# State tables transposed between two gate projections, state products ahead of output products, other PSUM banks

## Chip, cores and metric

The kernel runs on one core of one Trainium2 chip. The metric is the device time of one execution in microseconds (us), from the runs shown below; lower is better.

## The reference

Two blocks in sequence on x (512 tokens, 1024 wide). The first is a mixer (gated linear recurrence plus a Fourier mix) and a mixture of 16 experts with chosen tokens. The second, where the change lies, is

```python
h = rms_norm(x, norm_gain)
q, k, v, z_a, u, z_s, g_a, g_s = split(h @ w_in)         # g_a, g_s get a bias
y_a = (band_attention(q, k, v, rel_bias) * silu(z_a)) @ w_attn_out
y_s = gelu(s5_ssm(u, ...))     # 32 groups of 16 channels, 64 complex diagonal states each
y_s = glu(y_s @ w_glu + b_glu)
y_s = (y_s * silu(z_s)) @ w_ssm_out
x = x + (sigmoid(g_a) * y_a + sigmoid(g_s) * y_s) @ w_out
return rms_norm(x, final_gain)
```

## The kernel before

**Place in the program.** The mixer and the experts come first; the second block starts late. After the projections of u, q, k and v, TensorE (PE) runs a loop of 12 steps (L1147). Step i computes two gate projections, `gate{2i}` and `gate{2i+1}`. These are z_a, z_s, g_a and g_s in slices of 128 columns. A projection is 24 matmuls (L696 to L698: for each of eight tiles of 128 rows, low part by high, high by low, high by high). The two projections of a step share one unit of weights.

**Work between the gates.** The attention of a pair of heads and the state-space model of a quarter `c` of its channels (128 of 512) are spread over steps 0 to 8:

- At the end of an odd step p: `pair_probs` (probabilities transposed), `ssm_lags` (L1106, product `lags_p`), `pair_values`, `pair_scores` of the next pair.
- At the end of an even step with c = i/2: `ssm_tables(c)` (L1097, eight 128x128 transposes of the input table `wext` into `st_re_c` and `st_im_c`, not in step 0), `ssm_out(c-1)` (L1131, output products of the quarter before, into `ssm{c-1}`), `ssm_states(c)` (L1117, 32 small products into `state{c}`). In step 8 only `ssm_out(3)` remains.

**The other engines follow orders of their own, written out by hand.** ScalarE (ACT) in step i: high part of the next unit of weights (`weights_hi`, L1219); in an even step the eight exponentials of a pair of heads (L1443); the tanh of both gates (L1453, or L1459 for g_a and g_s); in an odd step the copies of the transposed probabilities; in an even step `state_rows` (L1432, two copies of the transposed tables from PSUM to `st`) and then the copy of `ssm{c}` to `ybuf` (L1203). VectorE (DVE) in an even step: scaling and maxima of the scores, normalisation, low part of the next unit of weights (`weights_lo`, L1657), and for z_a and z_s the product of each gate with its tanh (L1660), which frees the bank of that gate. In an odd step DVE begins with `states(c)` (L2113, rotation, scans, and the writes to `hbd` that `ssm_out` reads), then `weights_lo`, the gates, `lag_rows` and the next input table. GpSimd (POOL) waits until `ssm{c}` is done, computes the next output table `wc` (L1604 to L1609), issues eight DMAs of `ybuf` (L1631), waits for `lagsb`, sends it to DRAM (L1618) and reads it back as `toep` (L1622), which the next `ssm_out` needs.

**Banks.** The class `Jobs` (L105) gives each product one of eight PSUM banks and counts the uses of each. On PE `start(name)` waits until every earlier use of that bank has been read. Steps 0 to 7 name their banks explicitly. From step 8 on the gates take banks in turn, and the turn is set there:

```python
            if i == HEADS:
                jobs.turn = 6
```

So `gate16` has bank 6, `gate17` 7, `gate18` 0, `gate19` 1 and `gate20` 2. Before the change `st_re_c` and `st_im_c` had banks 0 and 1, `ssm{c}` bank 2 and `state{c}` bank 3. In step 8 ACT waits for `ssm3` ahead of the tanh of `gate16`, because its target `gsT` overlaps what `ssm_out` reads:

```python
                        if j == KT:
                            full(act_e, f"ssm{CT - 1}")
                        read(name, act_e.activation(dst, src, ACT.Tanh, scale=0.5, bias=hbias[:, 24 + j:25 + j]))
```

Of the kernel before, what the change touches and what calls it, by code (L numbers as in the profile page):

```python
# [41 lines left out]
CT = LRU // P  # L42
# [10 lines left out]
HEADS, DH = 8, 64  # L53
# [82 lines left out]
def build(nc, x, cols_d, cst_d, wbd_d, w_in, dft_s, w_out, w_gate, w_up, w_down, gf_d, w_in2, relp,  # L136
          bc_d, w_glu, w_ao, w_so, w_out2, gfin_d, out, u_dram, y_dram, x_dram, l_dram):
    with ExitStack() as ctx:
# [272 lines left out]
        for i in range(STEPS):  # L411
            odd, (one, other) = i % 2, ((6, 7), (7, 6))[i // 2 % 2]
            if i == HEADS:
                jobs.turn = 6
            for n in range(2):
                at = ((one, 5) if i else (5, one), (other, 5))[odd][n]
                jobs.add(f"gate{2 * i + n}", at if i < HEADS else None, M + 8 + i if n else None)
            if odd and i < HEADS:
                p = i // 2
                for a, b, at in ((0, 0, 0), (1, 0, 3), (0, 1, 1), (1, 1, 4), (0, 2, 2), (1, 2, one)):  # L420
                    jobs.add(f"probT{2 * p + a}_{b}", at)
                jobs.add(f"lags_{p}", other)
                jobs.add(f"pv{p}", 5)
                if p + 1 < PAIRS:
                    for b in range(6):
                        jobs.add(f"score{p + 1}_{b}", b if b < 5 else one)
            if not odd and i <= HEADS:
                c = i // 2
                if 0 < c < CT:
                    for n, name in enumerate(("st_re", "st_im")):  # L430
                        jobs.add(f"{name}_{c}", n)
                if c:
                    jobs.add(f"ssm{c - 1}", 2)
                if c < CT:
                    jobs.add(f"state{c}", 3)

        last_units = [("ao", 0), ("glu", 0), ("glu", 4), ("ao", 4), ("so", 0), ("so", 4)]
        for u, (what, n0) in enumerate(last_units):
# [77 lines left out]
        def both(unit, inner):  # L516
            return view_r(hi_of(unit), inner), view_r(ring_r[slot_of(unit)], inner)
# [145 lines left out]
        def _(pe):  # L663
# [483 lines left out]
            for i in range(STEPS):  # L1147
                unit = M + 8 + i
                split(unit)
                for n in range(2):  # L1150
                    project(f"gate{2 * i + n}", both(unit, 256), n * P, h_both, KT)
                if i % 2 == 1 and i < HEADS:
                    p = i // 2
                    pair_probs(p)
                    ssm_lags(p)
                    pair_values(p)
                    if p + 1 < PAIRS:
                        pair_scores(p + 1)
                if i % 2 == 0 and i <= HEADS:
                    c = i // 2  # L1160
                    if 0 < c < CT:
                        ssm_tables(c)
                    if c:
                        ssm_out(c - 1)
                    if c < CT:
                        ssm_states(c)
            operands = {"ao": ("za", (za_hi, za_lo)), "glu": ("y", (y_hi, y_lo)), "so": ("ys", (ys_hi, ys_lo))}
            for u, (what, n0) in enumerate(last_units):
                tile, rows = operands[what]
# [6 lines left out]
        def _(act_e):  # L1176
# [255 lines left out]
            def state_rows(c):  # L1432
                for ri, name in enumerate(("st_re", "st_im")):
                    copy_out(f"{name}_{c}", flat(st[:, ri, :, :]))

            state_rows(0)
            for i in range(STEPS):
                weights_hi(M + 9 + i)
                if i % 2 == 0 and i < HEADS:
                    for a in range(2):  # L1440
                        for q in range(TT):
                            act_e.wait_ge(max_ready, TT * (i + a) + q + 1)
                            act_e.activation(att_tile(a, q), att_tile(a, q), ACT.Exp, bias=top_of(a, q),  # L1443
                                             accum_out=sum_of(a, q)).then_inc(exp_ready, 1)
                for n in range(2):
                    name, g = f"gate{2 * i + n}", 2 * i + n
                    full(act_e, name)
                    src = bank[jobs.bank(name)][:, :]
                    if g < 2 * CT:
                        dst = (zaT if g < CT else zsT)[:, g % CT, :]  # L1450
                        if g == CT:
                            act_e.wait_ge(slot_x2_out, 16)
                        act_e.activation(dst, src, ACT.Tanh, scale=0.5).then_inc(th_ready, 1)  # L1453
                    else:
                        j = g - 2 * CT
                        dst = (gaT if j < KT else gsT)[:, j % KT, :]
# [3 lines that stand above are left out]
                if i % 2 == 1 and i < HEADS:  # L1460
                    for b in range(3):
                        w, at = (4, 3, 3)[b] * P, (0, 4, 7)[b] * P
                        for h in (i - 1, i):
                            name = f"probT{h}_{b}"
                            copy_out(name, pTs[h % 2][:, at:at + w], bank[jobs.bank(name)][:, 0:w])
                if i % 2 == 0 and 0 < i < HEADS:
                    state_rows(i // 2)
                if i % 2 == 0 and 0 < i <= HEADS:
                    c = i // 2 - 1
                    if c:  # L1470
                        act_e.wait_ge(y_out, 16 * T8 * c)
                    copy_out(f"ssm{c}", flat(ybuf))
                if i == HEADS:
                    act_e.wait_ge(states_ready, CT)
                    for c in range(CT):
                        was_read(act_e, f"pv{c}")
                        tile_hi(za_hi[:, c, :], zaT[:, c, :])
                if i in (GELU_STEP, GELU_STEP + 1):
                    cs = range(2 * (i - GELU_STEP), 2 * (i - GELU_STEP) + 2)
                    for c in cs:  # L1480
                        act_e.wait_ge(ygelu_in, c + 1)
                        act_e.activation(tmp[:, c % 2, :], tmp[:, c % 2, :], ACT.Tanh, scale=GELU_C).then_inc(ytanh, 1)
                    for c in cs:
                        act_e.wait_ge(y_ready, c + 1)
                        tile_hi(y_hi[:, c, :], yT[:, c, :])
# [161 lines left out]
        def _(dve):  # L1647
# [8 lines left out]
            def tt(out_, a, b, op):  # L1656
                return dve.tensor_tensor(out_, a, b, op)  # L1657
# [455 lines left out]
            def states(c):  # L2113

                cs = slice(c * CGP, (c + 1) * CGP)
                name = f"state{c}"
                full(dve, name)
                b = bank[jobs.bank(name)]
                vr, vi = (b[:, i * 256:(i + 1) * 256].rearrange("p (g j) -> p g j", g=CGP) for i in range(2))
                t0, t1, t2, t3 = (tmp[:, i // 2, i % 2 * 256:i % 2 * 256 + 256].rearrange("p (g j) -> p g j", g=CGP)  # L2120
                                  for i in range(4))
                rc, rs = rotc[:, cs, :], rots[:, cs, :]
                tt(t0, vr, rc, ALU.mult)
                tt(t1, vi, rs, ALU.mult)
                tt(t2, vi, rc, ALU.mult)
                tt(t3, vr, rs, ALU.mult).then_inc(bank_read[jobs.bank(name)], 1)
                was_read(dve, name)
                tt(t0, t0, t1, ALU.add)
                link(tt(t2, t2, t3, ALU.subtract))
                for g in range(CGP):  # L2130
                    dc = mag8[:, c * CGP + g:c * CGP + g + 1].to_broadcast([P, NCH])
                    dve.tensor_tensor_scan(t1[:, g, :], dc, t0[:, g, :], 0.0, ALU.mult, ALU.add)
                    last = dve.tensor_tensor_scan(t3[:, g, :], dc, t2[:, g, :], 0.0, ALU.mult, ALU.add)
                link(last)

                tt(t0, t1, rc, ALU.mult)
                link(tt(t2, t3, rs, ALU.mult))
                for a in range(2):
                    q = slice(64 * a, 64 * a + 64)
                    last = tt(hbd[q, 0, :, a, 1:NCH], t0[q, :, 0:NCH - 1], t2[q, :, 0:NCH - 1], ALU.subtract)  # L2140
                link(last)
                tt(t0, t1, rs, ALU.mult)
                link(tt(t2, t3, rc, ALU.mult))
                for a in range(2):
                    q = slice(64 * a, 64 * a + 64)
                    last = tt(hbd[q, 1, :, a, 1:NCH], t0[q, :, 0:NCH - 1], t2[q, :, 0:NCH - 1], ALU.add)
                last.then_inc(states_ready, 1)
                dve.wait_ge(states_ready, c + 1)
# [237 lines left out]
```

## Time and profile before

| | |
|---|---|
| median of 3 runs | 1488.29 us (1488.27 to 1488.67) |
| profiled execution, its own time | 1488.95 us |
| its span, first to last instruction | 1487.1 us |
| mean granted TensorE clock | 0.993 |
| busy PE, DVE, ACT, POOL | 92%, 37%, 22%, 8% |
| steps 0 to 8 of the gate loop | 1181.7 to 1331.8 us of the span |

Times in the rows are microseconds from the start of the span. A row of the timeline gives start, duration, engine, line, operation, output<-inputs, shape and, after x, how many instructions were merged; in brackets stands the idle time of that engine ahead of it and what ended it. A line such as L1657 or L1660 on DVE and L1203 on ACT is that of a helper, so the tile tells which operation it is.

### The profile page before, as it was taken

The numbers are of one execution on the slowest core, as the hardware profiler recorded it, in microseconds if no ns is written. First come the engines' busy times: TensorE is split into PE (matmuls) and PEld (weight loads), VectorE is DVE, ScalarE is ACT, GpSimd is POOL, SyncE is SP. The second block draws the span as 40 slices with busy tenths as digits, with TensorE's granted clock in tenths as the row PEclk, the third lists the DMA queues.
The fourth block names the chain that finished last, engine by engine and source line by source line (L and its number), as shares of the span: only waits on it lengthen the run. The fifth ranks groups of instructions, "written<-read, shape, count | busy, mean of one in ns | idle before, by whom it ended". The sixth has DMA issues, their size and how long they took to land.

```text
span 1487.1 us, 16564 instructions
## 1 busy us (share of the span) xinstructions
PE 1373.9 (92%) x6685; PEld 742.0 (50%) x6685; DVE 553.0 (37%) x980; ACT 320.0 (22%) x503; POOL 122.2 (8%) x204
## 2 busy tenths in 40 slices
PE   7999599999998998988988989889899999999997
PEld 6778233343332332332323323324378777888875
DVE  6675501211120121101201201113268698856663
ACT  5883100010010010000000100103042344433322
POOL 2000000000000000000000000002021314550001
PEclk9999899999999999999999999999999999999999
DMA  9126899999999999999999999999976123353321
GB/s 343 27 89 250 355 422 399 429 427 429 427 427 429 429 428 427 429 429 430 427 429 429 430 427 427 428 429 429 404 233 159 57 83 92 92 170 131 99 99 57
DMA packets 67603, 466.86 MB, mean 314 GB/s; under 512 B 5728, under 2 KB 30560, under 8 KB 42592
## 3 DMA queue, kind: packets, MB, share of 16 engines
q1 hardware_dynamic: 62720, 454.71, 74.4%
q0 software_dynamic: 4544, 10.98, 3.0%
q8 instruction: 36, 0.59, 0.2%
q10 hardware_dynamic: 288, 0.45, 0.1%
q14 instruction: 15, 0.12, 0.0%
HBM read 458.03 MB, written 7.05 MB: 313 GB/s over the span
## 4 chain that ended last, share of the span: by engine, by line
PE 59%; DMA 32%; DVE 4%; ACT 3%; issue 2%; POOL 0%; DVEq 0%; POOLq 0%; ACTq 0%
PE bank L930 12%; DMA wide<-in_w_up 11%; PE bank L981 10%; PE bank L696 8%; DMA early<-in_w_down 8%; PE bank L698 8%; PE bank L697 8%; DMA early<-in_w_up 7%; DMA wide<-in_w_down 5%; PE bank L876 3%; PE bank L1017 2%; PE bank L956 1%; PE bank L1093 1%; PE bank L726 1%; PE bank L736 0%
## 5 line engine op out<-in xcount | busy, mean ns | idle before, releaser
L930 PE MATMUL bank<-wide,xinT 128*64 128x512 f32 x1376 | 307.2, 596 | 43.5 <-DMA wide<-in_w_up 24.5
L930 PEld LDWEIGHTS bank<-wide,xinT 128*64 128x64 f32 x1376 | 96.4, 137 | 249.9 <-issue 169.9
L1660 DVE SCALAR_TENSOR_TENSOR th<-th,bank 128x512 f32<-128x512 f32 x32 | 20.6, 684 | 406.0 <-ACT th L1379 406.0
L930 PE MATMUL bank<-early,xinT 128*64 128x512 f32 x656 | 147.2, 596 | 20.7 <-DMA early<-in_w_up 11.8
L981 PE MATMUL bank<-wide,actT 128*64 128x512 f32 x656 | 145.0, 594 | 4.6 <-issue 3.4
L696 PE MATMUL bank<-hT_lo,ring_r 128*128 128x512 f32 x352 | 138.6, 394 | 2.2 <-ACT gt L1251 1.1
L698 PE MATMUL bank<-hT_hi,ring_r 128*128 128x512 f32 x352 | 137.1, 389 | 0.0
L697 PE MATMUL bank<-hT_hi,ring_r 128*128 128x512 f32 x352 | 137.0, 389 | 0.0
L1379 ACT ACTIVATE th<-bank 128x512 f32<-128x512 f32 x32 | 17.4, 594 | 496.9 <-PE bank L930 496.9
L1657 DVE TENSOR_TENSOR ring_r<-ring,ring_r 128x2048 fp32r<-128x2048 f32 (+1 forms) x39 | 87.2, 2237 | 55.7 <-ACT ring_r L1219 55.5
L930 PEld LDWEIGHTS bank<-early,xinT 128*64 128x64 f32 x656 | 45.9, 137 | 120.1 <-issue 79.3
L981 PEld LDWEIGHTS bank<-wide,actT 128*64 128x64 f32 x656 | 50.5, 137 | 92.1 <-issue 81.1
L1657 DVE TENSOR_TENSOR xinT<-bank,cols 128x512 f32<-128x512 f32 x16 | 11.1, 691 | 211.3 <-PE bank L893 211.3
L1219 ACT ACTIVATE ring_r<-ring 128x2048 fp32r<-128x2048 f32 x37 | 70.8, 1914 | 62.0 <-PE bank L698 31.6
L981 PE MATMUL bank<-early,actT 128*64 128x512 f32 x352 | 78.4, 595 | 2.4 <-issue 1.8
L696 PEld LDWEIGHTS bank<-hT_lo,ring_r 128*128 128x128 f32 x352 | 66.0, 188 | 21.3 <-issue 5.4
L698 PEld LDWEIGHTS bank<-hT_hi,ring_r 128*128 128x128 f32 x352 | 66.1, 188 | 14.0
L697 PEld LDWEIGHTS bank<-hT_hi,ring_r 128*128 128x128 f32 x352 | 66.1, 188 | 13.3
L1657 DVE TENSOR_TENSOR nrm<-nrm,bank 128x512 f32<-128x512 f32 x112 | 68.2, 680 | 6.5 <-PE bank L1017 6.5
L1550 POOL TENSOR_SCALAR stat<-stat 128x1 f32<-128x1 f32 x4 | 0.8, 189 | 809.8 <-ACT act L1370 809.5
L876 PE MATMUL bank<-xres,sel 128*64 128x512 f32 x256 | 57.7, 592 | 0.8 <-issue 0.8
L1017 PE MATMUL bank<-eo,gselT 64*128 64x512 f32 x240 | 56.7, 600 | 1.0
(408 smaller groups left out, 1653.5 us busy)
## 6 DMA issues: line engine op xcount, KB each, us to landing
wide<-in_w_gate SPq DMA_DIRECT2D x43, 2048.0 KB, 38.6
wide<-in_w_up SPq DMA_DIRECT2D x42, 2048.0 KB, 38.6
wide<-in_w_down SPq DMA_DIRECT2D x39, 2048.0 KB, 38.4
early<-in_w_down SPq DMA_DIRECT2D x22, 2048.0 KB, 38.5
early<-in_w_up SPq DMA_DIRECT2D x21, 2048.0 KB, 39.1
early<-in_w_gate SPq DMA_DIRECT2D x20, 2048.0 KB, 40.1
ring<-in_w_in SPq DMA_DIRECT2D x25, 1024.0 KB, 5.5
ring<-in_w_out SPq DMA_DIRECT2D x8, 1024.0 KB, 4.9
```

Of the source, the lines that this page charges most:

```text
L696: pe.matmul(dst, a[0], b[1], start=first, stop=False)
L697: pe.matmul(dst, a[1], b[0], start=False, stop=False)
L698: return pe.matmul(dst, a[0], b[0], start=False, stop=last)
L726: pe.matmul(bank[jobs.bank(name)][:, :], w_top[:, k, n * P:(n + 1) * P], hT_hi[:, k, :], start=(k == order[0]), stop=False)
L876: last = pe.matmul(bank[b][CAP * q:CAP * q + CAP, :], sel[:, t, :], rows[:, t, 512 * q:512 * q + 512], start=(t == 0), stop=(t == TT - 1 a ...
L930: last = pe.matmul(bank[1 + 2 * (m % 2) + q // 2][o:o + 64, :], xinT[:, k, :], w[:, i, q * 512:(q + 1) * 512], start=(k == 0), stop=(k == ...
L981: last = pe.matmul(bank[7][64 * n:64 * n + 64, :], actT[:, j // 2 * 4 + i, at:at + 64], w[:, i, n * 512:n * 512 + 512], start=(j == 0 and ...
L1017: pe.matmul(bank[b][:, :], gselT[64 * n:64 * n + 64, t, :], eo[64 * n:64 * n + 64, :], start=True, stop=True).then_inc(bank_full[b], 1)
L1219: act_e.activation(hi_of(unit), used(unit, ring[slot_of(unit)]), ACT.Copy).then_inc(w_hi, 1)
L1379: act_e.activation(th[:, b, :], bank[1 + b][:, :], ACT.Tanh, scale=0.5).then_inc(tanh_ready, 1)
L1657: return dve.tensor_tensor(out_, a, b, op)
L1660: return dve.scalar_tensor_tensor(out_, a, s, b, op0, op1)
```

## The change

- PE transposes the state tables of quarter c between the two gate projections of the even step, after `gate{2i}` and ahead of `gate{2i+1}`.
- After the second gate the state products come first and the output products after them.
- `st_re_c` and `st_im_c` go to banks 2 and 4, `state{c}` to bank 1, `ssm{c}` to bank 0.
- ACT copies the transposed tables between the tanh of the two gates.
- DVE waits for `ssm{c-1}` before it writes `hbd` in `states(c)`.

```diff
@@ banks of an even step
                 if 0 < c < CT:
                     for n, name in enumerate(("st_re", "st_im")):
-                        jobs.add(f"{name}_{c}", n)
+                        jobs.add(f"{name}_{c}", (2, 4)[n])
+                if c < CT:
+                    jobs.add(f"state{c}", 1)
                 if c:
-                    jobs.add(f"ssm{c - 1}", 2)
-                if c < CT:
-                    jobs.add(f"state{c}", 3)
+                    jobs.add(f"ssm{c - 1}", 0)
@@ PE
                 for n in range(2):
                     project(f"gate{2 * i + n}", both(unit, 256), n * P, h_both, KT)
+                    if n == 0 and i % 2 == 0 and 0 < i < HEADS:
+                        ssm_tables(i // 2)
...
                 if i % 2 == 0 and i <= HEADS:
                     c = i // 2
-                    if 0 < c < CT:
-                        ssm_tables(c)
+                    if c < CT:
+                        ssm_states(c)
                     if c:
                         ssm_out(c - 1)
-                    if c < CT:
-                        ssm_states(c)
@@ ScalarE
                 for n in range(2):
+                    if n and i % 2 == 0 and 0 < i < HEADS:
+                        state_rows(i // 2)
                     name, g = f"gate{2 * i + n}", 2 * i + n
...
-                if i % 2 == 0 and 0 < i < HEADS:
-                    state_rows(i // 2)
@@ VectorE, states(c)
                 link(tt(t2, t3, rs, ALU.mult))
+                if c:
+                    full(dve, f"ssm{c - 1}")
                 for a in range(2):
```

## Rows read from the trace of the kernel before

**Rows 1.** Who waited for whom on PE, 1180 to 1487: total us, times, longest.
```profile
PE bank L696 <- DVE ring_r L1657: 1.3, 2, 0.8
PE bank L1113 <- DVE zsT L1660: 0.8, 1, 0.8
```

**Rows 2.** Timeline of PE: transposes of probabilities and lags, step 3, then step 5.
```profile
1240.89 0.60 PE L1079 MATMUL bank<-cst,att_a 128*128 128x128 f32 x4
...
1244.07 0.65 PE L1113 MATMUL bank<-wc,bbd 128*32 128x128 f32 x16 [0.84 <-DVE zsT L1660]
...
1276.97 0.60 PE L1079 MATMUL bank<-cst,att_a 128*128 128x128 f32 x4
...
1279.25 0.64 PE L1113 MATMUL bank<-wc,bbd 128*32 128x128 f32 x16
```

**Rows 3.** Timeline of DVE: states(0) in step 1, states(1) in step 3.
```profile
1195.74 0.42 DVE L1657 TENSOR_TENSOR tmp<-bank,rotc 128x256 f32<-128x256 f32 x1
...
1202.92 2.29 DVE L1657 TENSOR_TENSOR ring_r<-ring,ring_r 128x2048 fp32r<-128x2048 f32 x1
...
1226.44 1.28 DVE L1660 SCALAR_TENSOR_TENSOR zsT<-zsT,bank 128x512 f32<-128x512 f32 x2
1229.98 0.42 DVE L1657 TENSOR_TENSOR tmp<-bank,rotc 128x256 f32<-128x256 f32 x1 [2.26 <-PE bank L1127]
...
1241.04 2.29 DVE L1657 TENSOR_TENSOR ring_r<-ring,ring_r 128x2048 fp32r<-128x2048 f32 x1
1243.25 1.28 DVE L1660 SCALAR_TENSOR_TENSOR zsT<-zsT,bank 128x512 f32<-128x512 f32 x2
```

**Rows 4.** Timeline of PE: the block at the end of step 2.
```profile
1224.24 1.04 PE L1103 MATMUL bank<-cst,wext 128*128 128x128 f32 x8
1225.12 0.39 PE L1138 MATMUL bank<-hbd,wc 128*128 128x128 f32 x2
...
1228.78 1.15 PE L1127 MATMUL bank<-ubuf,st 128*64 128x64 f32 x32
1229.87 0.50 PE L696 MATMUL bank<-hT_lo,ring_r 128*128 128x512 f32 x1
```

**Rows 5.** Timeline of PE: eight transposes inside another projection, first block.
```profile
143.35 1.03 PE L746 MATMUL bank<-cst,xres 128*128 128x128 f32 x8
...
144.46 0.39 PE L697 MATMUL bank<-hi,mix_lo 128*128 128x512 f32 x1
144.68 0.39 PE L698 MATMUL bank<-hi,hT_hi 128*128 128x512 f32 x1
```

**Rows 6.** Timeline of ACT, step 2: tanh of gate4, copies of the tables.
```profile
1222.28 0.58 ACT L1453 ACTIVATE zsT<-bank 128x512 f32<-128x512 f32 x1
...
1224.94 1.08 ACT L1203 ACTIVATE st<-bank 128x512 f32<-128x512 f32 x2
```

**Rows 7.** Timeline of POOL: last operation of a table, step 3; its DMAs, step 7.
```profile
1238.24 0.39 POOL L1609 TENSOR_TENSOR wc<-wc,relb 128x64 f32<-128x64 f32 x1
...
1315.87 0.59 POOL L1618 DMA_DIRECT2D l_scratch<-lagsb  x1 [1.82 <-DVE lagsb L2158]
1320.12 4.33 POOL L1622 DMA_DIRECT2D toep<-l_scratch  x8 [3.66 <-DMA l_scratch<-lagsb]
```

**Rows 8.** Timeline of PE, then of ACT: end of step 8, start of step 9.
```profile
1328.36 0.38 PE L1138 MATMUL bank<-hbd,wc 128*128 128x128 f32 x2
...
1331.84 0.48 PE L696 MATMUL bank<-hT_lo,ring_r 128*128 128x512 f32 x1
...
1332.19 1.26 ACT L1459 ACTIVATE gsT<-bank,hbias 128x512 f32<-128x512 f32 x2 [12.68 <-PE bank L1142]
1333.34 0.60 ACT L1203 ACTIVATE ybuf<-bank 128x512 f32<-128x512 f32 x1
```

**Rows 9.** PE's first matmuls after its longest late wait; stretch around them, clock seventh.
```profile
168.31 5.31 PE L688 MATMUL bank<-xres,cst 128*128 128x512 f32 x6 [9.63 <-DVE score L1863]
...
160.50:176.00 15.50, 6.79 (x16) 2.73 (x18) 13.68 (x27) 0.22 (x1) 0.00 (x0) 0.59 1.01 430
```

## Prediction

> **What bounds the kernel now.** The change lies in steps 0 to 8 of the gate loop, so I read the waits of PE from there to the end first. Two entries make 2.1 us [rows 1]; what is left out is smaller. PE is the bound of this stretch: an instruction moved on another engine gains only if it ends one of these waits, and a wait put on PE is paid in full. The reader should see how little there is to win. Only one entry can be touched by a reordering of the even step: the lag products of step 3 (L1113) waited for DVE's read of a gate. The waits on `ring_r` are for low halves of weights, one of them in step 0, where the change moves nothing but a bank and one near the end.
>
> Next I read the timeline around that wait. From the first transpose of probabilities to the lags PE took 1244.07 - 1240.89 = 3.18 us in step 3 and 1279.25 - 1276.97 = 2.28 us in step 5, with the same instructions [rows 2]. So the wait is worth 0.90 us, and only in step 3: from step 5 on the gates are g_a, which ACT reads and DVE doesn't. Its cause stands on DVE. `states(1)` could not begin before 1229.98, after 2.26 us of idleness, because the state products came last in PE's step 2; low weights followed at 1241.04 and the gate at 1243.25 [rows 3].
>
> **The change, part by part.**
>
> *State products first.* In step 2 the block after the gates is transposes 0.88 us, output products 3.66 us, state products 1.09 us (the differences of the starts in [rows 4]). With the transposes in mid-step and the state products first, these end 1.09 us after 1225.12 in place of 1229.87, at about 1226.2. The gates as a whole end 0.88 us later, which is in this figure. DVE is busy with the two products of gates until 1226.44 + 1.28 = 1227.72 [rows 3], so `states(1)` starts there, 2.3 us earlier. Everything behind it on DVE moves up by as much: low weights from 1238.8, first gate read by about 1241.7. PE wants its bank at 1240.89 + 2.28 = 1243.17. The wait is gone with 1.4 us to spare. **Term 1: -0.90 us.** What is late next there? POOL's table `wc`, which the lags need too. It starts when the output products end, now 1.09 us later, so it ends at 1238.63 + 1.1 = 1239.7 [rows 7], still 3.4 us ahead of PE. At most the term is -0.9; at least 0, if something holds DVE (below).
>
> *DVE beside POOL.* `states` took 1202.92 - 1195.74 = 7.18 us in step 1, with POOL idle, and 1241.04 - 1229.98 = 11.06 us in step 3 beside POOL's table [rows 3]. I keep 11.06 us for the moved block, since it still overlaps most of that table. The Trainium skill, "SBUF — State Buffer", section "SBUF: two separate sides", says that a GpSimd operation which begins first holds the port pair shared with VectorE for its whole length, and a VectorE operation with two SBUF inputs is then blocked. The longer `states` of step 3 agrees in sign; its 3.9 us are well under the time of POOL's table, from the end of the output products at 1228.8 to 1238.6, 9.8 us [rows 4, 7]. If every POOL operation blocked DVE in full, term 1 would turn into a loss; the rows don't bear that out, and the sum doesn't use it.
>
> *Transposes in mid-step, steps 2, 4 and 6.* They sit between matmuls of another operand type, so PE changes type twice more per step. A nearby case: eight transposes inside an earlier projection took 144.46 - 143.35 = 1.11 us up to the second matmul behind them, less one interval of matmuls, 144.68 - 144.46 = 0.22, is 0.89 us [rows 5], what they took (0.88) ahead of the output products [rows 4]. **Term 2: 0.** Bounds: the first matmul behind a block is 0.1 us longer (0.50 and 0.48 [rows 4, 8] against 0.39 [rows 5]), three steps give +0.3. On the other side the output products took 3.48 us in step 8, where a gate follows them, against 3.66 us in step 2 [rows 8, 4]: -0.18 three times is -0.5.
>
> *ACT's copies in mid-step.* The tanh of gate4 ends at 1222.86 and the copies take 1.08 us, so the rows stand at 1223.9 [rows 6]. The state products want them at 1225.12: 1.2 us of cover, and the tanh of gate5 (possible from 1225.1) isn't delayed. The 3.66 us of output products that used to hide these copies are no longer ahead of the products; if ACT's exponentials ran 1.2 us later, PE would pay the excess. Steps 4 and 6 have nearly the same timeline. Cost 0.
>
> *The second gate ends 0.88 us later* in these steps, and with it frees its unit of weights for the next load on SP's queue. The high half of that load is made by ACT at the start of the odd step, but DVE turns it into the low half only after `states`, at 1238.8 by the above; several us of cover, cost 0.
>
> *POOL's queue.* Its DMAs of `ybuf` move 1.1 us back. In step 7 POOL had nothing to do for 1.82 us before `lagsb` went at 1315.87, so its DMAs of `ybuf` were out by 1314.05; `toep` was issued from 1320.12 to 1324.45 [rows 7]; `ssm_out(3)` starts at 1328.36 [rows 8]. Now the `ybuf` DMAs end at 1315.1, before `lagsb` is ready, but closer to it. If the landing of `lagsb` is put back by the full 1.1 us, `toep` is issued by 1325.6 and has 2.8 us to land. Cost 0, bound +0.5.
>
> *DVE's new wait for `ssm{c-1}`.* Output products end at about 1229.9, the first write to `hbd` comes some 8.5 us after 1227.7. Cost 0.
>
> *Banks in steps 2, 4 and 6.* Banks 2 and 4 hold scores of the first head, which DVE reads first, and bank 1 one that it reads last, as it did for `st_im`. Cost 0.
>
> *Bank 0 at the end of step 8.* This is the part that costs. `ssm3` moves from bank 2 to bank 0. The turn of banks gives `gate18`, PE's very next product, bank 0; bank 2 belonged to `gate20`, a whole step later. PE therefore stops after `ssm_out(3)` until ACT has copied `ssm3`. ACT does so third: it waits for `ssm3`, takes two tanh from 1332.19 and the copy from 1333.34, done at 1333.94 [rows 8]. In the kernel before, PE went on at 1331.84. With about 0.1 us from the end of a read to the matmul that it frees, as in step 3, PE resumes near 1334.05. **Term 3: +2.2 us**, bounds 2.1 and 2.4. PE waits only once more after that, for at most 0.8 us [rows 1], and that wait is for work that ACT and DVE do on products of PE, so it moves along and gives nothing back.
>
> **Sum.** -0.90 + 0 + 2.2 = +1.3 us. Against the profiled execution's own time, 1488.95 us (span 1487.1 and 1.85 around it), this is 1490.25; that execution is 0.66 us above the median, so I give 1488.29 + 1.3 = **1489.6 us**. With the bounds of the terms the change lies between -0.9 - 0.5 + 2.1 = +0.7 and +0.3 + 2.4 - 0.7 = +2.0 us. No change within 0.2% (3.0 us) can be told from none here.
>
> **Rivals.**
>
> *A. The copy of `ssm3` is in time and no bank is waited for.* Then only term 1 is left: 1487.4 us. Against it: the order of uses of bank 0 leaves no other reading. 5%.
>
> *B. The stop lowers PE's clock: slower.* PE would stand still for 2.2 us at 1331.84. The trace has a stretch where the granted clock fell to the lower of its two levels: around PE's 9.63 us wait the mean is 0.59, and the matmuls behind it ran 5.31 us [rows 9]. If PE came back at 1.2 GHz for as long, half of that, 2.7 us, would be lost on top: +4.0, 1492.3 us. It decides as soon as the 2.2 us stop is enough for the clock to fall. The wait of 0.84 us in step 3 sits in a stretch at full clock, and the stop here is much nearer to that than to 9.63 us, with dense work on both sides. The Trainium skill, "TensorE: Matmul & The Clock Gate", section "Why this matters for your kernels", warns that an idle gap between bursts of matmuls takes the clock back to half; by that rule the 2.7 us would come on top of any gap long enough, and the trace here agrees for its 9.63 us wait alone. 5%.
>
> *C. `toep` or the table rows are late.* POOL's DMAs delay `lagsb` by more than I allow, or ACT's exponentials end late: +0.5 to +1.5 on top, 1490.1 to 1491.1 us. 8%.
>
> *D. The change doesn't do what it says.* DVE, slowed by POOL, still reads the gate late in step 3: term 1 vanishes, 1490.5 us. 5%.
>
> **How the numbers follow.** Forecast 77%, A, B, D 5% each, C 8%. The forecast's own range is 1489.0 to 1490.3; 0.6 us more on each side for the scatter of executions (the profiled one stands 0.66 off) gives 1488.4 to 1490.9, and C and D reach up to 1491.1. I take 1487.9 to 1491.4, which leaves out A and B and a little of the rest. Slower by over 0.2% (above 1491.27) is B and the tail of C: 8%. Faster by over 0.2% (below 1485.3) has no case with a mechanism: 2%. Same: 90%.
>
> **What would show it.** In the changed kernel's waits of PE, the entry on `zsT` at L1113 is gone and a new one of about 2.2 us stands at L696, ended by ACT's copy to `ybuf`. `states(1)` starts close behind the gates' products on DVE. The transposes take 0.88 us inside the step, the state products follow the gate without a wait, and the output products end the block. The clock stays at full through step 9. A stop at step 9 of another size, a wait on `st` at L1127, or a wait at the output products of step 8 would prove the sum wrong.

## The result, and the profile after

| | before | after |
|---|---|---|
| median | 1488.41 us (8 runs) | 1492.62 us (8 runs, 1490.73 to 1493.48) |
| ratio, 95% interval | | 1.0022 (1.0014 to 1.0031) |
| span of the profiled execution | 1487.1 us | 1491.5 us |

The change costs 4.2 us by the medians, 2.1 to 4.6 us by the interval of the ratio. The forecast was +1.3 us, 1489.6, with a range from 1487.9 to 1491.4; the direction was right, the size was wrong, and the measured time lies outside the range. Two executions of the later sets (4988.82 us in experiment 9 and 1778.63 us of the kernel before beside its last run) were disturbed and are left out of the ratios.

Waits of PE from 1180 us to the end, after the change:

```profile
PE bank L696 <- ACT ybuf L1203: 2.0, 1, 2.0
PE bank L696 <- DVE ring_r L1657: 1.3, 2, 0.9
PE bank L696 <- ACT st L1203: 0.3, 1, 0.3
```

Against [rows 1] the wait of L1113 is gone and a new one stands at the top, on ACT's copy to `ybuf`: the bank of `gate18`. Its place in the timeline of PE, after the change:

```profile
1332.15 0.44 PE L1142 MATMUL bank<-hbd,wc 128*128 128x128 f32 x2
1334.59 0.47 PE L696 MATMUL bank<-hT_lo,ring_r 128*128 128x512 f32 x1 [2.00 <-ACT ybuf L1203]
...
1335.71 0.63 PE L697 MATMUL bank<-hT_hi,ring_r 128*128 128x512 f32 x1
1336.14 0.63 PE L698 MATMUL bank<-hT_hi,ring_r 128*128 128x512 f32 x1
...
1339.24 0.40 PE L697 MATMUL bank<-hT_hi,ring_r 128*128 128x512 f32 x1
1339.47 0.40 PE L698 MATMUL bank<-hT_hi,ring_r 128*128 128x512 f32 x1
```

From 1335.71, about 1 us after PE resumes, its matmuls start 0.43 us apart, and later 0.23 again. The stretches of the same trace say why; each row is a stretch, its length, the busy time of PE, PE's weight loads, DVE, ACT and POOL with their instructions, then the granted clock, the DMA share and GB/s:

```profile
1334.00:1335.00 1.00, 0.41 (x2) 0.40 (x3) 0.00 (x1) 1.00 (x3) 0.26 (x1) 1.00 1.01 406
1335.00:1336.00 1.00, 1.00 (x5) 0.81 (x4) 1.00 (x2) 1.00 (x3) 1.00 (x3) 0.72 1.04 418
1336.00:1337.00 1.00, 1.00 (x4) 0.71 (x4) 1.00 (x3) 1.00 (x3) 1.00 (x3) 0.50 1.02 410
1337.00:1338.00 1.00, 1.00 (x4) 0.81 (x3) 0.50 (x1) 1.00 (x1) 1.00 (x3) 0.50 1.02 406
1338.00:1339.00 1.00, 1.00 (x4) 0.78 (x3) 0.65 (x1) 0.32 (x1) 0.93 (x2) 0.57 0.96 316
1339.00:1340.00 1.00, 1.00 (x6) 0.82 (x5) 1.00 (x1) 0.00 (x0) 0.00 (x0) 1.00 0.42 70
```

The clock is at 1.2 GHz from 1335.4 to 1338.9, some 3.4 us, in which PE did half of what it does at 2.4 GHz. PE is "busy" in every slice from 1335 on: busy shares don't show a slow clock, the durations do.

Both traces split by the starts of steps on PE, from `pair_scores(0)` to the last matmul:

| stretch | before, us | after, us | difference |
|---|---|---|---|
| scores and steps 0, 1 | 35.34 | 35.46 | +0.12 |
| steps 2, 4, 6 together | 49.95 | 50.21 | +0.26 |
| step 3 | 19.44 | 18.56 | -0.88 |
| steps 5, 7 | 34.72 | 34.69 | -0.03 |
| step 8, to the first matmul of `gate18` | 14.52 | 16.96 | +2.44 |
| `gate18` to the last matmul | 144.74 | 146.40 | +1.66 |
| sum | 298.71 | 302.28 | +3.57 |

The other 0.8 us of the difference of the spans lies ahead of `pair_scores(0)` (1177.87 and 1178.71), where nothing was changed. That start moved between 1177.5 and 1179.8 over the profiles of this study, with the waits of PE on expert weights; it is scatter, and the reason why small effects are read from starts inside the second block here.

### The profile page after: what moved, and what is told of

The parts are those of the page before. It is cut to its first block, busy times and chain, and to the rows that moved or that the text cites. A ratio compares the mean times of both kernels' runs of the same rounds, so it can differ in the third digit from the quotient of the medians.

```text
span 1491.5 us, 16567 instructions
## 1 busy us (share of the span) xinstructions
PE 1377.3 (92%) x6685; PEld 743.8 (50%) x6685; DVE 557.4 (37%) x980; ACT 320.2 (21%) x503; POOL 127.2 (9%) x204
## 4 chain that ended last, share of the span: by engine, by line
PE 60%; DMA 32%; DVE 3%; ACT 3%; issue 1%; POOL 0%; DVEq 0%; POOLq 0%; ACTq 0%
PE bank L930 12%; DMA wide<-in_w_up 10%; PE bank L981 10%; PE bank L696 8%; PE bank L698 8%; PE bank L697 8%; DMA early<-in_w_down 8%; DMA early<-in_w_up 7%; DMA wide<-in_w_down 5%; PE bank L876 3%; PE bank L1017 2%; PE bank L956 1%; PE bank L1093 1%; PE bank L1079 1%; PE bank L726 1%
```

## Experiments

Two statements were to be told apart: that bank 0 and the clock behind it are the whole loss, or that the moved transposes, or VectorE beside GpSimd, carry it. And what the reordering is worth by itself. The kernel before ran again beside each set: 1489.32 us with experiments 1 to 4, 1489.19 with 5 to 7 and the first run of 9, 1489.33 (one execution) with 8, 1489.60 with the last run. Its median moved by 0.9 us from the first set, so compare kernels of different sets by their ratios; the changed kernel has 1.0022.

**1. ssm3 alone back in bank 2.**

```diff
-                    jobs.add(f"ssm{c - 1}", 0)
+                    jobs.add(f"ssm{c - 1}", 0 if i < HEADS else 2)
```

> The changed kernel with one edit: ssm3, in step 8, goes back to bank 2; quarters 0 to 2 stay in bank 0. Theory (the stop on bank 0 and the clock that fell behind it are the whole loss): the 2.0 us wait on ybuf at L696 is gone, the clock stays at its upper level through steps 8 and 9, the run is 2.4 + 1.7 us faster than the changed kernel, so 1488.0 to 1488.7 us, level with the kernel before. Rival (the moved transposes, or VectorE beside GpSimd, cost the time): it stays at 1491 us or more. Rival (the thin matmuls of the output products lower the clock, not the stop): the wait goes, the low stretch stays, 1490.2 us.

Measured: 1489.00 us beside 1489.32 for the kernel before, ratio 0.9997 (0.9988 to 1.0006). One bank number gives back all of the loss. The waits of PE from 1180 to 1345, this kernel:

```profile
PE bank L696 <- DVE ring_r L1657: 0.7, 1, 0.7
PE bank L696 <- ACT st L1203: 0.3, 1, 0.3
PE bank L1138 <- issue: 0.2, 1, 0.2
```

From `pair_scores(0)` to the last matmul it takes 1178.42 to 1476.80, 298.38 us: 0.33 less than before. By these two profiles the order as such is a small gain, not the 0.9 that its one removed wait is worth (the ratio can't tell it from none); the third line is a part of what eats it (experiment 9).

**2. The kernel before, with only ssm3 in bank 0.**

```diff
-                    jobs.add(f"ssm{c - 1}", 2)
+                    jobs.add(f"ssm{c - 1}", 2 if i < HEADS else 0)
```

> The kernel before with one edit: ssm3, in step 8, goes to bank 0. Theory: the wait on ybuf appears at the start of step 9, 2.0 us idle and 2.3 to 2.4 us from start to start, and the clock falls for 3.4 us behind it in most executions: 1488.4 + 2.3 + 1.7 = 1492.4 us. If the clock doesn't fall with this order of work: 1490.7. Rival (the loss needs the new order of the even steps): 1488.4 us.

Measured: 1493.46 us, ratio 1.0025 (1.0015 to 1.0035), +4.1 us. PE in this kernel:

```profile
1332.06 0.44 PE L1142 MATMUL bank<-hbd,wc 128*128 128x128 f32 x2
1334.49 0.47 PE L696 MATMUL bank<-hT_lo,ring_r 128*128 128x512 f32 x1 [2.00 <-ACT ybuf L1203]
...
1336.11 0.63 PE L698 MATMUL bank<-hT_hi,ring_r 128*128 128x512 f32 x1
```

The same stop and the same slow matmuls, without any of the reordering. With experiment 1 this settles from both sides that the bank is the cause; experiments 3 and 4 separate the stop from the clock.

**3. The copy of ssm3 ahead of the two tanh.** In step 8 of ScalarE `copy_out("ssm3")` moves from behind the loop over the two gates to its front; bank 0 stays.

> The changed kernel with ScalarE's copy of ssm3 ahead of the two tanh of step 8 instead of behind them; bank 0 stays. Theory: PE's stop shrinks by two tanh, 1.2 us, to 0.8 us idle, and a stop as short as the others of this trace leaves the clock up: 1492.6 - 1.2 - 1.7 = 1489.7 us. Rival (any stop behind the output products lowers the clock): 1491.4 us.

Measured: 1490.15 us, ratio 1.0005 (0.9996 to 1.0014). PE's timeline in this kernel, and below it the stretch from 1332 to 1345 with the granted clock third from the end:

```profile
1333.03 0.47 PE L696 MATMUL bank<-hT_lo,ring_r 128*128 128x512 f32 x1 [0.84 <-ACT ybuf L1203]
```

```profile
1332.00:1345.00 13.00, 12.16 (x55) 9.96 (x55) 4.79 (x5) 7.13 (x11) 5.52 (x10) 1.00 0.71 255
```

The stop is 1.16 us shorter and the kernel 2.5 us faster than the changed one, by the medians and by the ratios: the clock, 1.00 from 1332 to 1345, gives back the rest.

**4. Work in the stop.** Ahead of `gate18`:

```diff
+                if i == HEADS + 1:
+                    b = start(f"gate{2 * i + 1}")
+                    for _ in range(8):
+                        pe.matmul(b[:, :], hT_hi[:, 0, 0:P], hT_hi[:, 1, :], start=True, stop=True)
```

> The changed kernel with eight matmuls (128x128 by 128x512) whose result is never read, into bank 1, between the output products of step 8 and gate18, about 1.8 us of work inside the stop of 2.0 us. Theory: the stop costs the same from ssm_out(3) to gate18 (2.4 us), but PE is hardly idle and the clock stays at its upper level, so only the 1.7 us of the low clock go: 1490.9 us. Rival (the clock falls for the work before the stop, not the stop): 1492.6 us, low stretch still there.

Measured: 1491.06 us, ratio 1.0011 (1.0002 to 1.0020). PE's timeline in this kernel, and below it the same stretch as in experiment 3:

```profile
1333.28 2.07 PE L1152 MATMUL bank<-hT_hi 128*128 128x512 f32 x8
1335.52 0.47 PE L696 MATMUL bank<-hT_lo,ring_r 128*128 128x512 f32 x1 [0.17 <-ACT ybuf L1207]
```

```profile
1332.00:1345.00 13.00, 12.83 (x64) 10.55 (x63) 4.79 (x5) 6.32 (x9) 5.51 (x10) 1.00 0.75 254
```

`gate18` starts as late behind the output products as in the changed kernel: 1335.52 - 1333.09 = 2.43 us behind the start of the last L1142, 2.44 in the changed kernel. But it runs at full speed, and eight useless matmuls make the kernel 1.6 us faster (1.0011 against 1.0022): from `gate18` to the last matmul 1335.52 to 1480.31, 144.79 us, against 146.40 in the changed kernel and 144.74 before. The stop and the clock are two terms, and this measures the second alone.

**5. A stop in between.** The copy goes between the two tanh.

> The changed kernel with ScalarE's copy of ssm3 between the two tanh of step 8: a stop between that of the changed kernel (2.0 us idle) and that with the copy first (0.84 us idle), about 1.4 us idle and 1.8 us from start to start. It asks where the clock falls. Theory: the cost is the stop alone as long as the clock stays, 1490.15 (copy first) + 0.6 = 1490.7 us; if 1.4 us is enough for the clock to fall, 1.7 us more, 1492.4. The longest wait in the kernel before with the clock up is 1.9 us, so I expect it to stay up.

Measured: 1490.16 us, ratio 1.0009 (1.0000 to 1.0018). The stop in the profile:

```profile
1334.65 0.47 PE L696 MATMUL bank<-hT_lo,ring_r 128*128 128x512 f32 x1 [1.42 <-ACT ybuf L1203]
```

From this matmul to 1345 the profile grants the full clock. Nine of the eleven executions took 1489.7 to 1491.8 us with a mean clock of 0.993 or 0.994, two took 1493.9 and 1494.4 with 0.991. A fall in those two fits the numbers, but they have no trace, so that is not shown, nor at which stop it would have come (experiment 6 shows a fall in the experts). In the same way seven of eight executions of the changed kernel lie between 1492.3 and 1493.5 at 0.992 and one at 1490.73 and 0.993.

**6. Output products ahead of the state products again** (bank 2 for ssm3, transposes still between the gates).

> The version with ssm3 in bank 2, and the output products ahead of the state products again; transposes stay between the gates. It separates the two halves of the reordering. Theory: the gain of the change comes from the early state products only, so the wait of the lags on VectorE in step 3 comes back (0.8 to 0.9 us) and the step's block costs the same: 0.9 us slower than with ssm3 in bank 2 and the new order. Rival (the new order gains nothing): same time as that version, no wait at L1113.

Measured: 1490.02 us, ratio 1.0004 (0.9995 to 1.0014). The wait is back, in this kernel's timeline of PE:

```profile
1244.38 0.65 PE L1113 MATMUL bank<-wc,bbd 128*32 128x128 f32 x16 [0.83 <-DVE zsT L1660]
```

Step 3 takes 1230.17 to 1249.62, 19.45 us, as before the change (19.44). The early state products are what removes the wait.

The same profile has something else to show. In the experts PE waits for weights behind a block of 16 matmuls; here, and then at the same place in the profile of experiment 1:

```profile
1050.60 3.65 PE L930 MATMUL bank<-wide,xinT 128*64 128x512 f32 x16 [0.45 <-DMA wide<-in_w_up]
1056.32 5.35 PE L930 MATMUL bank<-wide,xinT 128*64 128x512 f32 x16 [2.07 <-DMA wide<-in_w_gate]
```

```profile
1051.23 3.65 PE L930 MATMUL bank<-wide,xinT 128*64 128x512 f32 x16 [0.51 <-DMA wide<-in_w_up]
1057.04 3.65 PE L930 MATMUL bank<-wide,xinT 128*64 128x512 f32 x16 [2.16 <-DMA wide<-in_w_gate]
```

Behind 2.07 us the granted clock falls and the same 16 matmuls take 5.35 us, 1.7 us more; behind 2.16 us it stays at full (1.00 from 1057.04 to 1063.04) and they take 3.65. A stop of about 2 us can lower the clock, and its length alone doesn't decide it.

**7. Transposes at the end of the step** (bank 2 for ssm3, state products first).

> The version with ssm3 in bank 2, state products first, but the tables are transposed at the end of the step, right ahead of the state products. Theory: the transposes were put between the gates because ScalarE's copies (tanh of the second gate 0.6 us, then 1.08 us) would otherwise lie open ahead of the state products: PE waits about 0.9 us in each of steps 2, 4 and 6, +2.7 us against the version with ssm3 in bank 2. Rival (mid-step transposes aren't needed, the copies are hidden): within 0.5 us of that version.

Measured: 1491.89 us, ratio 1.0017 (1.0008 to 1.0027). PE's waits in this kernel, 1180 to 1345:

```profile
PE bank L1127 <- ACT st L1203: 3.2, 3, 1.1
PE bank L696 <- DVE ring_r L1657: 0.7, 1, 0.7
PE bank L696 <- ACT st L1203: 0.3, 1, 0.3
```

From `pair_scores(0)` to the last matmul it takes 1178.57 to 1479.74, 301.17 us, 2.8 more than experiment 1: ScalarE's copies lie open, 1.0 to 1.1 us in each of three steps. The change needs its mid-step transposes.

**8. GpSimd's table behind `states` of the next quarter** (bank 2 for ssm3). The edit, beside that of experiment 1:

```diff
                     full(pool, f"ssm{c}")
+                    pool.wait_ge(states_ready, c + 2)
                     output_table(c + 1)
```

> The version with ssm3 in bank 2, and GpSimd begins each output table only after states of the next quarter is through on VectorE. It measures what the overlap costs. Theory (GpSimd's table lengthens states): states(1), from its first operation to the low weights behind it, takes 7.2 us as in step 1 in place of 12.6 us; GpSimd's table itself then starts some 7 us later than now and PE waits for it at the lags of steps 3, 5 and 7, several us each, so the run is 5 to 15 us slower. Rival (states is long for its operands or PSUM reads, not for GpSimd): states(1) stays above 10 us.

One execution, 1498.67 us. `states(1)` on VectorE, from its first operation to the low weights, in the changed kernel:

```profile
1228.59 0.42 DVE L1657 TENSOR_TENSOR tmp<-bank,rotc 128x256 f32<-128x256 f32 x1
...
1236.18 1.28 DVE L1657 TENSOR_TENSOR tmp<-tmp,rots 128x256 f32<-128x256 f32 x1
...
1241.18 2.30 DVE L1657 TENSOR_TENSOR ring_r<-ring,ring_r 128x2048 fp32r<-128x2048 f32 x1
```

and with GpSimd kept off:

```profile
1227.27 0.41 DVE L1658 TENSOR_TENSOR tmp<-bank,rotc 128x256 f32<-128x256 f32 x1
...
1231.45 0.42 DVE L1658 TENSOR_TENSOR tmp<-tmp,rots 128x256 f32<-128x256 f32 x1
...
1234.46 2.29 DVE L1658 TENSOR_TENSOR ring_r<-ring,ring_r 128x2048 fp32r<-128x2048 f32 x1
```

12.59 us against 7.19: the same multiplication takes 1.28 or 0.42 us. GpSimd's table is the whole difference. That kernel pays with waits for the table, 6.1 us in three steps at L1113. The longest of them lowers the clock as well, here from 0.7 us before its end on; below it the stretch from there, with the granted clock third from the end:

```profile
1245.74 1.08 PE L1113 MATMUL bank<-wc,bbd 128*32 128x128 f32 x16 [2.80 <-issue]
```

```profile
1245.00:1252.00 7.00, 6.26 (x36) 2.95 (x38) 4.96 (x9) 1.91 (x1) 5.30 (x11) 0.51 0.34 63
```

Step 3 takes 24.27 us against 18.54 in experiment 1: 2.80 of waiting and some 2.9 of slow matmuls. The waits of 1.66 and 1.67 us in steps 5 and 7 leave the clock at full.

**9. Two waits taken away: a version faster than both.** Again bank 2 for ssm3, and in step 0 VectorE makes the low half of the next weights ahead of the normalisations.

```diff
                         scores_out(i // 2, a)
+                    if i == 0:
+                        weights_lo(M + 9 + i)
                     for a in range(2):
                         probabilities(i // 2, a)
...
-                weights_lo(M + 9 + i)
+                if i:
+                    weights_lo(M + 9 + i)
```

> The version with ssm3 in bank 2, and in step 0 VectorE makes the low half of the next weights ahead of the two normalisations of probabilities, while it waits for ScalarE's exponentials. Theory: PE's wait on the weights at the start of step 1 (0.7 to 0.9 us) goes too; against the kernel before, -0.87 (lags) -0.8 (weights) + 0.3 (steps a little longer) = -1.3 us, 1488.0 us beside 1489.3. Rival: VectorE is late for something else in step 1 and the wait only moves.

Measured: 1488.02 us beside 1489.19, ratio 0.9987 (0.9978 to 0.9996). PE waits on `ring_r` at the start of step 1 no more. But in step 7 of this kernel GpSimd shows what still goes wrong:

```profile
1308.74 2.23 POOL L1607 TENSOR_TENSOR wc<-pw_in,bc 128x64 f32<-128x64 f32 x1
...
1311.57 4.20 POOL L1631 DMA_DIRECT2D y_scratch<-ybuf  x8
1315.76 0.60 POOL L1618 DMA_DIRECT2D l_scratch<-lagsb  x1
1320.45 4.33 POOL L1622 DMA_DIRECT2D toep<-l_scratch  x8 [4.09 <-DMA l_scratch<-lagsb]
```

An operation of 0.30 us takes 2.23, with VectorE's low weights running from 1308.51 for 2.30 us; then the DMAs of `ybuf` hold `lagsb`, for which GpSimd had 1.82 us to spare before the change [rows 7]. The output products of step 8 start 11.27 us after the gates' start instead of 11.04. So the last run moves those DMAs, now in a function `rows_out(c)`, behind the one of `lagsb`:

```diff
+                if c:
+                    rows_out(c - 1)
                 pool.wait_ge(l_out, 16 * (c + 1))
...
-                was_read(pool, f"ssm{c}")
-                for t in range(T8):
-                    pool.dma_start(y_dram[c * P:(c + 1) * P, t, :].rearrange("(g c) j -> c g j", c=SG),
-                                   ybuf[t * SG:(t + 1) * SG, :, :]).then_inc(y_out, 16)
+            rows_out(CT - 1)
```

> The version with ssm3 in bank 2 and the early low weights in step 0, and on GpSimd the eight DMAs of ybuf of quarter c-1 move behind the DMA of lagsb of the next odd step, into the time in which that DMA is landing. Theory (GpSimd's queue makes toep late for the output products of step 8, since the new order puts its table and these DMAs later): lagsb goes as soon as VectorE has it, toep is issued some 2 us earlier in step 7, step 8's two gates take 11.04 us again instead of 11.2 to 12.2, and the run gains 0.1 to 1.2 us on the version without it, 1487.7 us beside 1489.2. Rival (toep is late for the DMA queue itself, in which the ybuf rows now stand between lagsb and toep): toep lands no earlier, step 8 keeps its 11.2 us or more.

Measured: 1487.78 us beside 1489.60, ratio 0.9989 (0.9980 to 0.9998). GpSimd's timeline in this kernel:

```profile
1313.84 0.62 POOL L1624 DMA_DIRECT2D l_scratch<-lagsb  x1 [2.51 <-DVE lagsb L2164]
1314.45 4.20 POOL L1617 DMA_DIRECT2D y_scratch<-ybuf  x8
1318.64 4.18 POOL L1630 DMA_DIRECT2D toep<-l_scratch  x8
```

Step 8's gates take 1315.29 to 1326.33, 11.04 us. From `pair_scores(0)` to the last matmul: 1177.45 to 1474.58, 297.13 us, 1.58 less than before the change and 0.38 less than without this edit (1177.70 to 1475.21). The two last versions can't be told apart by their times (1488.02 and 1487.78, ratios 0.9987 and 0.9989); the gain over the kernel before can.

## Why the prediction was wrong, point by point

- **Term 1, the wait in step 3: -0.90 forecast, -0.88 measured** (19.44 to 18.56 us). Right, but with the wrong margin. "The wait is gone with 1.4 us to spare" rested on `states` keeping its 11.06 us. It took 12.59, and of the 2.3 us by which it starts earlier VectorE kept 0.9: low weights 11.17 us after the step's start before (1241.04 - 1229.87), 10.28 us after (1241.18 - 1230.90). The lags start 2.31 us behind the first transpose, against 2.28 without any wait [rows 2]. The change earned just what it needed. Experiment 8 names the taker. The rule of the Trainium skill, "SBUF — State Buffer", section "SBUF: two separate sides", was set aside as not borne out in full; a GpSimd operation of 64 elements that waits out VectorE's 2.3 us (experiment 9) fits it, in the direction that I hadn't thought of: VectorE holding GpSimd.
- **Term 2, transposes in mid-step: 0 forecast, +0.26 us for three steps measured**, inside its bounds (+0.3).
- **ScalarE's copies: hidden, as forecast.** No wait at L1127. Experiment 7 shows the 3.2 us that they cost uncovered.
- **GpSimd's queue, "cost 0, bound +0.5":** partly wrong. The DMAs of `ybuf` were to be out at 1315.1, before `lagsb` is ready; they were out at 1317.81, with 1.93 us of the delay in that one operation (2.23 us instead of 0.30, in the changed kernel too), and `lagsb` went 1.9 us later (1317.80 against 1315.87). In the changed kernel's profile this costs 0.12 us at step 8 (11.16 against 11.04), in experiment 1 0.34, and in the profile of experiment 5 1.2 (1317.19 to 1329.42); in experiments 3 and 4, with the same order up to there, nothing (11.03 and 11.05). In all five the output products start 1.9 to 2.1 us behind the last issue of `toep`, against 3.9 before: the cover is used up. Rival C was given 8%; it came true in part, smaller than its +0.5 to +1.5 in all but one.
- **Term 3, bank 0: +2.2 forecast, +2.3 measured** (output products to `gate18` 5.80 us against 3.48 [rows 8]); with the line above this is the 2.44 of step 8.
- **Rival B, the clock, was what happened.** The step that failed: the sum priced the stop of PE at its length alone and the clock behind it at nothing, with 5% for the case that it falls. The runs show 3.4 us at 1.2 GHz and 1.7 us lost, in place of 0 (and of the 2.7 that the rival took from behind a far longer wait). The reason given was that 2.2 us lies nearer to 0.84, which leaves the clock up, than to 9.63. But the trace of the kernel before had waits between them that weren't read: 1.57 and 1.60 us in the experts (930.79 and 1056.43) with the clock at full behind them, and 1.91 us just ahead of the 9.63; below it a stretch with the granted clock third from the end:

```profile
158.08 0.60 PE L860 MATMUL bank<-cst,aff 128*16 128x128 f32 x4 [1.91 <-DVE aff L1657]
```

```profile
159.00:160.00 1.00, 0.00 (x0) 0.00 (x0) 0.66 (x1) 0.31 (x1) 0.00 (x0) 0.83 0.96 410
```

  The clock falls at 159.7, when PE had waited 1.91 us, worked 0.6 and waited 1.0 again; the low level of [rows 9] needed no 9.63 us. These rows gave no reason for so small a chance.
- **The sum and its bounds.** Added to the forecast, +1.3 and +1.7 make +3.0. The measured split has +3.57, the rest being term 2 and about 0.1 us each in term 3, at `toep` and in steps 0 and 1; the medians' 4.2 holds 0.6 more, which no trace places; it is within the scatter of the part ahead. The upper bound of +2.0 counted term 1 as -0.7 and left out GpSimd's +0.5, although the text had bounded term 1 at 0. With both it is +3.2, 1491.5 us, and the measured 1492.62 lies outside still: no bound of a term held the clock.
- **The Trainium skill, "TensorE: Matmul & The Clock Gate", section "Why this matters for your kernels",** was cited for a gap long enough to lower the clock. The traces show it for 2.00 us idle here, in both profiles that have that stop, for 2.80 us in experiment 8 and for 2.07 us in experiment 6; not for 1.42, 0.84 or 0.17 us at this place in one profile each, nor for 2.11 and 2.16 us in the experts in the profile of experiment 1. What besides the length decides isn't shown: PE's work ahead of the stop was the thin output products here and full blocks of 16 matmuls in the experts, where it went both ways.

## What to carry to other kernels

When a product gets another bank, follow that bank to its next user, above all across the point where an explicit assignment hands over to a turn: the one number for ssm3 made the next product of PE wait for an engine that had two other things to do first. A stop of PE can cost more than its length: look up the granted clock behind every stop of about that length in the trace, price the case that it falls, and give it a real chance. One stop of that length with the clock up doesn't rule it out: here 2.16 us left it up and 2.00 and 2.07 us didn't. If the stop can't be avoided, shorten it by reordering the engine that frees the bank, or fill it.

## What was not expected of the hardware

A stop of 2.00 us in a stretch that PE otherwise fills lowered the granted clock to 1.2 GHz about 1 us after PE had resumed, for 3.4 us; with 1.42 us the clock stayed up in the profile, but it stayed up behind 2.16 us elsewhere too. VectorE and GpSimd slowed each other both ways: `states` 7.19 us alone and 12.59 beside GpSimd's table, and a GpSimd operation of 0.30 us held for 2.23 us by one of VectorE's. Beside the same table `states` took 11.06 us before and 12.59 after a shift of one to two microseconds, and the small operation was held in the new order only, so a duration taken from one order of work isn't safe for another.
